# Cross attention's keys and the memory's norm made during setup, between the first modulation's quarters

## The chip, the cores and the metric

The kernel runs on one core of a Trainium2 chip. The metric is the device time of one launch in microseconds. The engines are TensorE (PE), VectorE (DVE), ScalarE (ACT), GpSimd (POOL) and SyncE (SP), which here only issues DMAs.

## The reference

A batch of one sequence with S = 512 tokens and D = 1024 channels goes through two transformer blocks and then a third one of another kind:

- Block 0: modulated RMS norm, a sparse attention mixer (NSA), a squared-ReLU MLP. Block 1: the same with a sliding-window attention. The modulation is `mod = silu(c) @ ada_w[i] + ada_b[i]`, cut into shift, scale and gate twice: `h = rms_norm(x) * (1 + scale) + shift`.
- Second part: `x += hybrid_mixer(rms_norm(x))`, `x += cross_attention(rms_norm(x), m)`, `x += conv_ffn(rms_norm(x))`, and a last norm.

What the change is about is the first modulation and this:

```
m = rms_norm_2(mem, norm_mem_w)            # mem: 256 rows of 1024, an input
q = h @ wq;  k, v = split(m @ wkv)         # 4 heads of 256
probs = softmax(q k^T * 256**-0.5);  x += (probs v) @ wo
```

`m`, `k` and `v` depend on inputs alone, not on x.

## The kernel before, in words

Activations lie transposed: channels on partitions in DC = 8 chunks of 128, tokens along the row. Every projection is made in float32 accuracy from two float32r parts. Weights come in units of 128 output channels x 1024 (512 KB). For each unit SP fetches `raw` (`units`, the transfer at L626), ACT makes the high part `wh` (L2634, `highs`), POOL the low part `wl` (L808), and PE makes three products a chunk: high x high, low x high, high x low (`products`, L915 to L917): 24 matmuls. `raw`, `wh` and `wl` are rings of RING = 4 slots. Results go to PSUM banks 0 to 3 in turn and are read out by DVE or ACT; the order of units is fixed by the list STAGES (L41). Every engine runs its own list in order, and semaphores (`wait_ge`, `then_inc`) tie them together. A wait on SP, ACT or POOL holds everything listed behind it.

**Setup.** SP loads positions, constants, x, and the 16 pieces of the first modulation's weights (each 128 input channels x 1024, for shift and for scale) before and around the first four units (L686 to L698). PE makes half of the scale with 128x128 weights and one moving column (`scale_part`, L1284); DVE accumulates the other half and the shift, 1024 columns an operation (L1879 to L1895); PE sums the partitions with a column of ones. ACT squares x, PE sums the squares (`square_sums`), and PE spreads the inverse root over the partitions (`root_spread`). DVE makes the rotary angles (`angle`), ACT their sines. Then the first norm: DVE scales a chunk (L1772), ACT adds the shift and rounds it to the high part `ah` (L2693), DVE makes the low part `al` (L1790). PE takes the chunks as they come, for three units at once (`gemm_first`, L969, which stores at L978, L979, L983); from the fourth unit on it goes unit by unit.

**Mixer's output and cross attention.** The memory (`me`, 1 MB) is fetched during the mixer's output projection (`gemm_squared` of mix_out, L1464). Its norm stands between that projection's units in four engines (`memory` in the PE, DVE and ACT lists): squares on ACT, sum on PE, root on ACT, scaling on DVE, high part `mh` on ACT, low part `ml` on DVE. Then PE makes the keys `xk`, one unit at a time with 256 columns: two around the residual's sum of squares, five after it, then three pairs of units with the memory as the weights (`gemm_pairs`: values `xv`), then the last key. Beside them DVE and ACT make the norm of x for the queries (`norm("xq", ...)`, L1772 and L1788). The query units follow; the last two value units are made inside the heads' loop.

Of the kernel before, what the change touches and what calls it, by code (L numbers as in the profile page):

```python
# [13 lines left out]
P = 128  # L14
# [21 lines left out]
UNITS_KV = 16  # L36
# [4 lines left out]
STAGES = (("nsa_in", UNITS_NSA_IN), ("phi", UNITS_PHI), ("nsa_out", UNITS_OUT), ("mlp0", UNITS_MLP),  # L41
          ("swa_in", UNITS_SWA_IN), ("swa_out", UNITS_OUT), ("mlp1", UNITS_MLP),
          ("mix_in", UNITS_MIX_IN), ("mix_out", UNITS_OUT), ("xq", UNITS_Q), ("kv", UNITS_KV),
          ("xo", UNITS_OUT), ("ffn", UNITS_FFN))
FIRST = {}
_n = 0
for _name, _count in STAGES:
# [5 lines left out]
SMALL = (("ones", P), ("ident", P), ("prev", P), ("diag", P), ("cmp_add", SC * P),  # L53
         ("inv", 1), ("cT", DC), ("ada_b", 96), ("norm_g", 64), ("pe", 32), ("b1", 4), ("b2k", 1), ("b2v", HD),
         ("w2", 4 * HD), ("sinks", HEADS), ("norm_mix", DC), ("norm_xattn", DC), ("norm_mem", DC),
         ("norm_ffn", DC), ("norm_final", DC), ("pool_scale", 4), ("gk_b", 2), ("gla_norm", 1),
         ("conv_w", 3 * 44), ("conv_b", 44), ("pool_w", 4 * P), ("gk_w2", 256), ("invcnt", 4 * 16),
         ("tri", HD), ("quarter", 4))
# [15 lines left out]
def place_of_units():  # L74

    n = {name: FIRST[name] for name, _ in STAGES}
    of = list(range(UNITS))

    def stage(name, runs):
        got = [n[name] + a + k for a, count in runs for k in range(count)]  # L80
        of[n[name]:n[name] + len(got)] = got
# [7 lines left out]
    xattn = n["xq"]  # L89
    kv = n["kv"]  # L90
    of[xattn:xattn + UNITS_KV + UNITS_Q] = [*range(kv, kv + 13), kv + 15, *range(n["xq"], n["xq"] + UNITS_Q), kv + 14, kv + 13]
# [5 lines left out]
KV0, XQ0 = FIRST["xq"], FIRST["xq"] + UNITS_KV - 2  # L97
# [155 lines left out]
def build(nc, src, out):  # L253
# [105 lines left out]
    trscr = scratch("trscr", [P, 2, S])  # L359

# [27 lines left out]
    me = at("me", 48, [P, DC, MEM])  # L388
    mh = at("mh", w0 + 16, [P, DC, MEM], F32R)
    ml = at("ml", w0 + 24, [P, DC, MEM], F32R)  # L390
    msq = at("msq", w0 + 54, [P, DC, MEM])
# [25 lines left out]
    ada_in = [sem(f"ada_in{i}") for i in range(16)]  # L417
    first_in = sem("first_in")
    scale_part_made = sem("scale_part_made")
    scale_sum = sem("scale_sum")  # L420
    shift_made = sem("shift_made")
    cond_done = sem("cond_done")
    ada_first = sem("ada_first")
# [99 lines left out]
    gla_std = sem("gla_std")  # L523
    mem_sq = sem("mem_sq")
# [25 lines left out]
    NORMS = ("nsa_in", "mlp0", "swa_in", "mlp1", "mix_in", "mem", "xq", "ffn_plain", "ffn")  # L550
# [13 lines left out]
    MEM_CHUNKS = {4: (0, 1, 2), 5: (3, 4, 5), 6: (6, 7)}  # L564
# [18 lines left out]
    def first_place(c):  # L583
        return ps[:, (7, 3, 4)[c % 3]]
# [31 lines left out]
    def _(sp):  # L616
        early = slice(COL["inv"][0], COL["cT"][1])
        sp.dma_start(sm[:, early], src["small"][:, early]).then_inc(first_in, 16)
        sp.dma_start(pos_i[:], src["pos"]).then_inc(first_in, 16)
# [66 lines left out]
        for n in (0, 8):  # L686
            sp.dma_start(ada0[:, n], src["ada"][n]).then_inc(ada_in[n], 16)
        for part in (slice(0, early.start), slice(early.stop, SMALL_COLS)):
            sp.dma_start(sm[:, part], src["small"][:, part]).then_inc(small_in, 16)
        for n in (1, 9):  # L690
            sp.dma_start(ada0[:, n], src["ada"][n]).then_inc(ada_in[n], 16)
        sp.dma_start(x[:], src["xT"]).then_inc(x_in, 16)
        for n in (10, 2, 11, 3, 12, 13, 14, 15):
            sp.dma_start(ada0[:, n], src["ada"][n]).then_inc(ada_in[n], 16)
        units(0, 1)
        for n in (4, 5, 6, 7):
            sp.dma_start(ada0[:, n], src["ada"][n]).then_inc(ada_in[n], 16)
        units(1, RING)  # L698
# [6 lines left out]
        units(RING, 10)  # L705
# [9 lines left out]
        units(10, 11)  # L715
        sp.wait_ge(kc_kept, 16 * GROUPS)
        load_tokens(0)
        for n in range(2):
            sp.wait_ge(evac, 2 + n + 1)
            for i in range(2):  # L720
                sp.dma_start(cscr[1, 2 * n + i], vtmp[64 * i:64 * i + 64, n]).then_inc(vc_kept, 16)
        units(11, 12)
        sp.wait_ge(vc_kept, 16 * GROUPS)
        load_tokens(1)
        units(12, 14)
        store_k(0, 0)
        units(14, 16)
        store_k(1, 1)
        units(16, 18)
        store_q(2, 0)  # L730
        units(18, 22)
        store_q(3, 1)
        units(22, 26)
        store_q(4, 2)
        units(26, 30)
# [6 lines left out]
        units(30, 32)  # L742
# [3 lines left out]
        units(32, FIRST["nsa_out"] + RING)  # L746
# [21 lines left out]
        sp.wait_ge(t_made, 3 * DC)  # L768
# [35 lines left out]
    def _(pool):  # L804
# [53 lines left out]
        def low_of_norm(name, shift, c, high=ah, to=al):  # L858

            if shift:  # L860
                pool.wait_ge(shifted, len(POOL_LOWS) * NORMS[1:].index(name) + c // 2 + 1)
            else:
                pool.wait_ge(high_made, DC * NORMS.index(name) + c + 1)
# [36 lines left out]
    def _(pe):  # L900
# [68 lines left out]
        def gemm_first(first, high, low, name, between=None):  # L969
# [3 lines left out]
            pe.wait_ge(lo_done, first + 3)  # L973
            for k in range(DC):
                pe.wait_ge(high_made, DC * NORMS.index(name) + k + 1)
                for j in range(3):
                    o, slot = ps[:, (n + j) % RING], (first + j) % RING
                    nc.tensor.matmul(o, wh[:, slot, k], high[:, k], start=k == 0, stop=False)  # L978
# [36 lines left out]

        def square_sum(c, tokens=S):

            q = squares[0]
# [2138 lines left out]
```

## Time and profile before

| | us |
|---|---|
| median of 3 runs | 2034.01 (2033.76 to 2034.55) |
| the profiled execution's own time | 2034.94 |
| its span | 2033.1 |
| PE busy | 1969.2 (97%) |
| DVE busy | 1133.1 (56%) |
| POOL busy | 942.7 (46%) |
| ACT busy | 702.1 (35%) |

The span is the time from the first to the last recorded instruction; the execution's own time is a little longer. PE's busy time counts pipelined matmuls whose ends are modelled, so a busy PE need not be at its peak: how far apart matmuls start tells more. Between stages the DMA engines move 124 GB/s on average.

### The profile page before, as it was taken

The page shows a single profiled execution, that of the slowest core. Times are in us where ns is not written, and L with a number is a line of the kernel's source. Part 1 is how long each engine was busy: PE and PEld are TensorE (multiplying, and loading weights), DVE is VectorE, ACT ScalarE, POOL GpSimd, SP SyncE. Part 2 cuts the span into 40 slices and gives each one's busy share as a digit, 9 for nine tenths or more (in the row PEclk, how much of TensorE's full clock was granted, in tenths as well). Part 3 has the DMA queues.
Part 4 walks back from the last instruction along what each step waited for, and adds up shares of the span by engine and source line. Part 5 has one row for each costly group of instructions (what it writes and reads, how often), then busy time and mean ns, then how long its engine had stood idle before and what let it go on. Part 6 is the DMA issues. An engine that isn't in the chain of part 4 may idle for free.

```text
span 2033.1 us, 27246 instructions
## 1 busy us (share of the span) xinstructions
PE 1969.2 (97%) x10389; PEld 1625.4 (80%) x10389; DVE 1133.1 (56%) x1763; ACT 702.1 (35%) x1230; POOL 942.7 (46%) x552
## 2 busy tenths in 40 slices
PE   6999999999999999999999999999999999999998
PEld 5888776878888887877888888788897788888887
DVE  7575785873645567766322313786463368345164
ACT  3343564432222233554322223342343342222122
POOL 1465554465444445564544444542363245444442
PEclk9998999999999999999999999999999999999999
DMA  7775340645555523722332332222343223332331
GB/s 291 233 218 169 98 121 26 224 145 190 201 179 196 176 73 114 208 93 63 110 98 93 100 98 93 73 73 73 100 137 95 63 73 114 94 103 93 94 103 63
DMA packets 81590, 252.24 MB, mean 124 GB/s; under 512 B 12224, under 2 KB 14784, under 8 KB 81216
## 3 DMA queue, kind: packets, MB, share of 16 engines
q1 hardware_dynamic: 81472, 250.61, 38.2%
q8 instruction: 80, 1.31, 0.3%
q14 instruction: 38, 0.31, 0.0%
HBM read 235.21 MB, written 15.37 MB: 123 GB/s over the span
## 4 chain that ended last, share of the span: by engine, by line
PE 73%; issue 12%; POOL 7%; DVE 5%; ACT 3%; POOLq 0%; DVEq 0%; ACTq 0%
PE ps L915 20%; PE ps L916 20%; PE ps L917 20%; POOL wl L808 5%; PE ps L1201 2%; PE ps L1141 2%; ACT pr L2781 2%; PE ps L1173 1%; DVE st L1996 1%; PE ps L1478 1%; PE ps L1503 1%; POOL al L864 1%; PE ps L983 1%; POOL x L856 1%; PE ps L963 0%
## 5 line engine op out<-in xcount | busy, mean ns | idle before, releaser
L808 POOL TENSOR_TENSOR wl<-raw,wh 128x1024 fp32r<-128x1024 f32 x309 | 768.8, 2493 | 943.1 <-ACT wh L2634 942.8
L2634 ACT CAST wh<-raw 128x1024 fp32r<-128x1024 f32 x309 | 322.4, 1050 | 899.3 <-PE ps L917 832.4
L915 PE MATMUL ps<-ah,wh 128*128 128x512 f32 x904 | 357.5, 395 | 1.3 <-DVE pair L1926 1.3
L916 PE MATMUL ps<-ah,wl 128*128 128x512 f32 x904 | 352.7, 390 | 0.0
L917 PE MATMUL ps<-al,wh 128*128 128x512 f32 x904 | 352.5, 390 | 0.0
L915 PE MATMUL ps<-hh,wh 128*128 128x512 f32 (+1 forms) x712 | 273.2, 384 | 2.0 <-DVE hl L2537 2.0
L916 PE MATMUL ps<-hh,wl 128*128 128x512 f32 (+1 forms) x712 | 272.1, 382 | 0.0
L917 PE MATMUL ps<-hl,wh 128*128 128x512 f32 (+1 forms) x712 | 272.0, 382 | 0.0
L915 PEld LDWEIGHTS ps<-ah,wh 128*128 128x128 f32 x904 | 170.3, 188 | 40.0 <-issue 2.6
L916 PEld LDWEIGHTS ps<-ah,wl 128*128 128x128 f32 x904 | 170.2, 188 | 35.9 <-issue 1.5
L917 PEld LDWEIGHTS ps<-al,wh 128*128 128x128 f32 x904 | 170.1, 188 | 35.8
L915 PEld LDWEIGHTS ps<-hh,wh 128*128 128x128 f32 x712 | 133.8, 188 | 29.8 <-DVE hl L2537 3.3
L917 PEld LDWEIGHTS ps<-hl,wh 128*128 128x128 f32 x712 | 133.9, 188 | 26.1
L916 PEld LDWEIGHTS ps<-hh,wl 128*128 128x128 f32 x712 | 133.9, 188 | 25.5
L915 PE MATMUL ps<-fh,wh 128*128 128x512 f32 x328 | 127.6, 389 | 0.0
L916 PE MATMUL ps<-fh,wl 128*128 128x512 f32 x328 | 127.6, 389 | 0.0
L917 PE MATMUL ps<-fl,wh 128*128 128x512 f32 x328 | 127.6, 389 | 0.0
L2781 ACT ACTIVATE pr<-ps,st 128x512 f32<-128x512 f32 (+1 forms) x192 | 94.0, 503 | 55.7 <-DVE st L1996 45.8
L2158 DVE TENSOR_SCALAR rs<-ps 128x512 f32<-128x512 f32 x64 | 44.1, 690 | 114.7 <-PE ps L917 109.7
L827 POOL TENSOR_SCALAR pr<-pr,st,gates 128x512 f32<-128x512 f32 (+3 forms) x128 | 81.0, 647 | 56.3 <-DVE st L2024 56.2
L1141 PE MATMUL ps<-ks,qs 128*128 128x256 f32 (+3 forms) x384 | 89.3, 340 | 5.6 <-ACT pr L2781 3.6
L2171 DVE TENSOR_TENSOR y<-ps,y 128x512 f32<-128x512 f32 x32 | 22.1, 691 | 125.7 <-PE ps L917 125.7
(419 smaller groups left out, 3270.2 us busy)
## 6 DMA issues: line engine op xcount, KB each, us to landing
raw<-in_units SPq DMA_DIRECT2D x309, 512.0 KB, 3.6
ada_mlp<-in_ada SPq DMA_DIRECT2D x64, 512.0 KB, 3.3
ada<-in_ada SPq DMA_DIRECT2D x16, 512.0 KB, 15.8
qs<-qscr SPq DMA_DIRECT2D x32, 256.0 KB, 3.3
ada_in<-in_ada SPq DMA_DIRECT2D x16, 512.0 KB, 3.7
ks<-kscr SPq DMA_DIRECT2D x24, 256.0 KB, 4.6
x<-in_xT SPq DMA_DIRECT2D x1, 2048.0 KB, 13.8
qscr<-rot_h SPq DMA_DIRECT2D x16, 128.0 KB, 2.3
```

The source lines that it names most:

```text
L808: nc.gpsimd.tensor_tensor(wl[:, slot], raw[:, slot], wh[:, slot].bitcast(F32), ALU.subtract).then_inc(lo_done, 1)
L827: op = nc.gpsimd.tensor_scalar(o, o, st[:, 2, n % 4, i:i + 1], gates[:, i, c:c + 1], ALU.mult, ALU.mult)
L856: nc.gpsimd.tensor_tensor(x[:, c], y[:, c], x[:, c], ALU.add).then_inc(x_new_pool, 1)
L915: nc.tensor.matmul(out_ap, wh[:, slot, k], high[:, k0 + k], start=first and k == 0, stop=False)
L916: nc.tensor.matmul(out_ap, wl[:, slot, k], high[:, k0 + k], start=False, stop=False)
L917: mm = nc.tensor.matmul(out_ap, wh[:, slot, k], low[:, k0 + k], start=False, stop=last and k == ks - 1)
L1141: nc.tensor.matmul(o, qs[:, Q_SLOT[j], i * P:(i + 1) * P], ks[:, slot, part, k0 * P:k1 * P], start=part == 0, stop=False)
L1201: mm = nc.tensor.matmul(ps[HD * h:HD * h + HD, bank, q[0] * P:(q[-1] + 1) * P], vv[:, kind, kb, col_v:col_v + HD], pt[:, n[h] % 4, place[k ...
L2158: link(v.tensor_scalar(rs[:, k % 2], b, 0.0, None, ALU.max))
L2171: v.tensor_tensor(y[:, c], bank(), y[:, c], ALU.add).then_inc(evac, 1)
L2634: a.copy(wh[:, slot], raw[:, slot]).then_inc(hi_done, 1)
L2781: a.activation(pr[:, n % 3, b * S + col:b * S + col + width], ps[:, plan.s_bank(w, b), col:col + width], ACT.Exp, bias=shift[:, i:i + 1], ...
```

## The change

- Units are reordered: stage `xk` (8 key units) comes first of all, ahead of `nsa_in`; only the 8 value units stay in cross attention.
- The table of constants is reordered, so that the first piece holds all that setup needs, and the memory is the second transfer.
- The memory's norm and the keys are made in setup, with the same operations as before, half of the squares now on DVE. Highs and lows of the memory (`mh0`, `ml0`) and the keys (`xk0`) are stored to DRAM (`mscr`, `xkscr`), and fetched back during mix_out.
- The first modulation is made otherwise: by quarters of 256 output channels, wholly on PE (`condition`): four input chunks side by side on column groups of 32, twice accumulated. ACT copies the bank (`rows`), PE transposes it (`turn_rows`), DVE adds the four parts (`first_coefs`). Quarters 0 and 1 stand between keys 4 and 7, quarters 2 and 3 inside the first group of the NSA gemm. The quarter's weights are fetched as runs of 256 floats.
- x's squares are summed by DVE (`first_square`) and once on PE, instead of chunk by chunk on PE.
- `gemm_first` of the first stage waits for its three units one by one.
- In cross attention `values` makes a pair of value units in two halves of 128 memory rows; the first pair stands around the residual's sum of squares.

```diff
@@ STAGES
+STAGES = (("xk", UNITS_K), *LAID[:10], ("xv", UNITS_V), *LAID[11:])
@@ SP, setup (the old order of loads is gone)
+        def ada_load_first(q):
+
+            if q == 3:
+                sp.wait_ge(rows_made, 1)
+            for w in (1, 0):
+                sp.dma_start(ada0[:, q % 3, w], src["ada"][DC * w:DC * w + DC, :, 256 * q:256 * q + 256].rearrange("k p m -> p k m")
+                             ).then_inc(ada_in[2 * q + w], 16)
+        units(0, 3)
+        sp.dma_start(pos_i[:], src["pos"]).then_inc(pos_in, 16)
+        sp.dma_start(x[:, 0:4], src["xT"][:, 0:4]).then_inc(x_half, 16)
+        sp.dma_start(x[:, 4:8], src["xT"][:, 4:8]).then_inc(x_in, 16)
+        units(3, 6)
+        ada_load_first(0)
+        units(6, 7)
+        ada_load_first(1)
+        units(7, NSA0 + 1)
+        ada_load_first(2)
+        nsa_units(1, 3)
+        ada_load_first(3)
+        nsa_units(3, 4)
+        for part, tile in enumerate((mh0, ml0)):
+            sp.dma_start(mscr[part], tile[:].bitcast(F32)).then_inc(mem_kept, 16)
+        sp.dma_start(sm[:, early.stop:], src["small"][:, early.stop:]).then_inc(small_in, 16)
+        nsa_units(4, 5)
         sp.wait_ge(trig_made, 2)
         sp.dma_start(trscr, ang[:, 4:6]).then_inc(trig_kept, 16)
+        sp.wait_ge(evac, UNITS_K)
+        sp.dma_start(xkscr, xk0[:]).then_inc(mem_kept, 16)
+        nsa_units(5, 6)
 
         sp.wait_ge(trig_kept, 16)
-        sp.wait_ge(t_made, DC)
+        sp.wait_ge(t_made, 2 * DC)
...
@@ SP, mix_out
-        units(FIRST["swa_out"] + RING, FIRST["mix_out"] + 6)
-        sp.wait_ge(pooled, 4)
-        sp.dma_start(me[:], src["memT"]).then_inc(x_in, 16)
-        units(FIRST["mix_out"] + 6, UNITS)
+        units(FIRST["swa_out"] + RING, FIRST["mix_out"] + 8)
+        sp.wait_ge(head_made, 4)
+        for part, tile in enumerate((mh, ml)):
+            sp.dma_start(tile[:].bitcast(F32), mscr[part]).then_inc(mem_back, 16)
+        units(FIRST["mix_out"] + 8, FIRST["mix_out"] + 12)
+        sp.wait_ge(unit_used, FIRST["mix_out"] + UNITS_OUT)
+        sp.dma_start(xk[:], xkscr).then_inc(keys_back, 16)
+        units(FIRST["mix_out"] + 12, UNITS)
@@ PE, setup
+        def condition(q):
+
+            for w in (1, 0):
+                pe.wait_ge(ada_in[2 * q + w], 16)
+                if q and w:
+                    pe.wait_ge(rows_read, q)
+                for r in range(2):
+                    for j in range(4):
+                        k = 4 * r + j
+                        mm = nc.tensor.matmul(ps[32 * j:32 * j + 32, 6, 256 * w:256 * w + 256],
+                                              cond[:, k:k + 1].to_broadcast([P, 32]), ada0[:, q % 3, w, k],
+                                              start=r == 0, stop=r == 1)
+            mm.then_inc(rows_made, 1)
+        def next_rows(k):
+
+            q = k // 2 + 2
+            if q < 4 and k % 2:
+                turn_rows(q)
+            elif q < 4:
+                condition(q)
...
+        for j in range(4):
+            keys(j)
+        sums_squared(spread_too=False)
+        keys(4)
+        root_spread(1)
         pe.wait_ge(cond_done, 1)
-        for k in range(2):
-            scale_part(k)
-        pe.wait_ge(setup_done, 1)
-        square_sums()
...
+        condition(0)
+        keys(5)
+        turn_rows(0)
+        keys(6)
+        condition(1)
+        keys(7)
+        turn_rows(1)
         u = FIRST["nsa_in"]
-        gemm_first(u, ah, al, "nsa_in")
+        gemm_first(u, ah, al, "nsa_in", between=next_rows, one_by_one=True)
@@ PE, cross attention
-        gemm_squared(FIRST["mix_out"], oh, ol, ready=(evac, done[0] - 8), between=memory)
-
-        gemm(KV0 + 2, 5, mh, ml, tokens=MEM)
-        gemm_pairs(KV0 + 7, 3, mh, ml, tokens=MEM)
-        gemm(KV0 + 13, 1, mh, ml, tokens=MEM)
+        def first_values(c):
+
+            if c == DC - 1:
+                pe.wait_ge(mem_back, 32)
+                values(V0, 0)
+            if c == DC:
+                values(V0, 1)
+        gemm_squared(FIRST["mix_out"], oh, ol, ready=(evac, done[0] - 8), between=first_values)
+
+        for pair in (1, 2):
+            for i in range(MC):
+                values(V0 + 2 * pair, i)
@@ DVE, setup
+        key_out(0)
         for step in range(4):
-            angle(0, step)
-        angle(1, 0)
...
+            angle(step // 4, step % 4)
+        key_out(1)
+        first_square(2)
+        first_square(3)
+        key_out(2)
+        for c in range(4, DC):
+            first_square(c)
+        sets[0] += 1
+        summed[0] += 1
+        key_out(3)
+        rms(1)
+        for step in range(4, 8):
+            angle(step // 4, step % 4)
+        key_out(4)
+        key_out(5)
@@ ACT, setup
+        highs(0, 1)
+        act.wait_ge(mem_sum, 1)
+        a.activation(rs[0:64, 0, 0:P], ps[0:64, 6, 0:P], ACT.Sqrt, bias=eps[0:64], scale=1.0 / D).then_inc(std_made, 1)
+        highs(1, 2)
+        for k in range(DC):
+            act.wait_ge(t_made, k + 1)
+            a.copy(mh0[:, k], me[:, k]).then_inc(high_made, 1)
+        normed[0] += 1
+        highs(2, 3)
+        for c in range(4):
+            first_square(c)
+        highs(3, 4)
+        for c in range(4, DC):
+            first_square(c)
+        summed[0] += 1
+        highs(4, 5)
+        act.wait_ge(sq_used, squared[0])
+        a.copy(sxx[:], ps[:, 4, 0:P])
+        root(1)
+        act.wait_ge(first_in, 16)
+        a.activation(cond[:], small("cT"), ACT.Silu).then_inc(cond_done, 1)
+        highs(5, 6)
         act.wait_ge(ang_done, 2)
         for h in range(2):
             a.activation(ang[:, 4 + h], ang[:, 4 + h], ACT.Sin).then_inc(trig_made, 1)
+        highs(6, 7)
+        keep_rows(0)
+        highs(7, 8)
+        for q in range(4):
+            act.wait_ge(shift_made, q + 1)
+            for c in (2 * q, 2 * q + 1):
+                act.wait_ge(t_made, DC + c + 1)
+                a.activation(ah[:, c], first_place(c), ACT.Identity, bias=mod[:, c:c + 1]).then_inc(high_made, 1)
+            if q == 0:
+                highs(8, 9)
+            if q < 3:
+                keep_rows(q + 1)
+            if q == 0:
+                highs(9, 11)
+        normed[0] += 1
+        highs(11, 12)
```

## Rows read from the trace of the kernel before

**Rows 1.** The page's busy times: share of the span and instructions.

```profile
PE 1969.2 (97%) x10389; PEld 1625.4 (80%) x10389; DVE 1133.1 (56%) x1763; ACT 702.1 (35%) x1230; POOL 942.7 (46%) x552
```

**Rows 2.** Busy time by stretch of setup: engine busy (instructions), granted clock, DMA share, GB/s.

```profile
30.00:44.00 14.00, 10.76 (x49) 10.50 (x49) 11.58 (x14) 4.97 (x6) 7.86 (x4) 1.00 0.67 267
44.00:63.00 19.00, 18.96 (x72) 15.47 (x73) 9.04 (x13) 4.49 (x7) 1.47 (x1) 1.00 0.36 139
```

**Rows 3.** Timeline of PE in setup: start, duration, line, operation, tiles, idle before.

```profile
37.58 3.57 PE L1094 MATMUL ps<-sm,acc 128*128 128x1 f32 x16 [0.21 <-DVE acc L1881]
...
44.60 0.63 PE L979 MATMUL ps<-ah,wl 128*128 128x512 f32 x1
45.03 0.63 PE L978 MATMUL ps<-ah,wh 128*128 128x512 f32 x1
...
61.62 0.39 PE L978 MATMUL ps<-ah,wh 128*128 128x512 f32 x1
61.84 0.39 PE L979 MATMUL ps<-ah,wl 128*128 128x512 f32 x1
...
63.20 0.39 PE L915 MATMUL ps<-ah,wh 128*128 128x512 f32 x1
```

**Rows 4.** x's load in the timeline, and the memory's load with its time to landing.

```profile
4.74 0.59 SPq L692 DMA_DIRECT2D x<-in_xT  x1
...
18.65 1.15 ACT L2644 ACTIVATE sq<-x 128x512 f32<-128x512 f32 x2 [14.41 <-DMA x<-in_xT]
...
me<-in_memT SPq DMA_DIRECT2D x1, 1024.0 KB, 5.6
```

**Rows 5.** Timeline of the memory's norm in the output projection (PE, ACT, DVE).

```profile
1445.70 1.32 ACT L2938 ACTIVATE msq<-me 128x256 f32<-128x256 f32 x4
1454.94 1.94 PE L998 MATMUL ps<-msq,sm 128*32 128x128 f32 x32
1456.69 1.28 ACT L2941 ACT_TABLE_LOAD   x1
1468.66 1.27 DVE L2436 SCALAR_TENSOR_TENSOR me<-me,sm,ps 128x256 f32<-128x256 f32 x3
```

**Rows 6.** Timeline of PE from the first key to the first query matmul.

```profile
1485.00 0.28 PE L915 MATMUL ps<-mh,wh 128*128 128x256 f32 x1
1485.11 0.28 PE L916 MATMUL ps<-mh,wl 128*128 128x256 f32 x1
...
1491.50 1.05 PE L1006 MATMUL ps<-rs,sm 128*128 128x128 f32 x8
1492.31 0.36 PE L915 MATMUL ps<-mh,wh 128*128 128x256 f32 x1
...
1527.48 0.40 PE L915 MATMUL ps<-ah,wh 128*128 128x512 f32 x1
```

**Rows 7.** Timeline of POOL and DVE in the query norm: POOL busy, then idle.

```profile
1490.05 21.21 POOL L808 TENSOR_TENSOR wl<-raw,wh 128x1024 fp32r<-128x1024 f32 x8 [6.70 <-ACT wh L2634]
...
1495.81 1.93 DVE L1788 TENSOR_TENSOR al<-tt,ah 128x512 fp32r<-128x512 f32 x1
...
1513.36 0.68 DVE L1788 TENSOR_TENSOR al<-tt,ah 128x512 fp32r<-128x512 f32 x1
```

**Rows 8.** The page's costliest groups: a unit's low and high.

```profile
L808 POOL TENSOR_TENSOR wl<-raw,wh 128x1024 fp32r<-128x1024 f32 x309 | 768.8, 2493 | 943.1 <-ACT wh L2634 942.8
L2634 ACT CAST wh<-raw 128x1024 fp32r<-128x1024 f32 x309 | 322.4, 1050 | 899.3 <-PE ps L917 832.4
```

**Rows 9.** Timeline of DVE in setup: first and last of eight angle operations.

```profile
5.02 0.43 DVE L1827 TENSOR_SCALAR ang<-ang 128x512 f32<-128x512 f32 x1
...
9.05 0.43 DVE L1840 TENSOR_SCALAR ang<-ang 128x512 f32<-128x512 f32 x1
```

**Rows 10.** Timeline of PE in the heads: four score matmuls, four transposes.

```profile
1539.33 1.99 PE L1478 MATMUL ps<-xk,xq 128*128 128x256 f32 x8 [0.78 <-DVE xq L2277]
1546.66 0.60 PE L1491 MATMUL ps<-sm,xp 128*128 128x128 f32 x4
```

More of the change, by code:

```diff
@@ L967, in gemm_pairs, with gemm_first @@
                 done[0] += tokens // P // 2
-        def gemm_first(first, high, low, name, between=None):
+        def gemm_first(first, high, low, name, between=None, one_by_one=False):
             n = done[0]
             bank_free(n + 2)
-            pe.wait_ge(lo_done, first + 3)
+            if not one_by_one:
+                pe.wait_ge(lo_done, first + 3)
             for k in range(DC):
@@ L977, in gemm_first @@
                     o, slot = ps[:, (n + j) % RING], (first + j) % RING
+                    if one_by_one and k == 0:
+                        pe.wait_ge(lo_done, first + j + 1)
                     nc.tensor.matmul(o, wh[:, slot, k], high[:, k], start=k == 0, stop=False)
@@ L1297, in _ @@
-        root_spread(1)
-        pe.wait_ge(scale_part_made, 4)
-        for m in range(8):
-            mm = nc.tensor.matmul(ps[:, 7, m:m + 1], acc1[:, m * P:(m + 1) * P], small("ones")[:, 0:1],
-                                  start=False, stop=m == 7)
-        mm.then_inc(scale_sum, 1)
-        pe.wait_ge(ada_first, 8)
-        ada(ps[:, 6, 0:8], acc0)
+        def condition(q):
[10 more added lines that the diff above has]
+            mm.then_inc(rows_made, 1)
@@ new lines, in turn_rows, with keys @@
+        def turn_rows(q):
+            pe.wait_ge(rows_kept, q + 1)
+            for i in range(4):
+                mm = nc.tensor.transpose(ps[:, 6, i * P:(i + 1) * P], rows[:, q % 2, i * P:(i + 1) * P], small("ident"))
+            mm.then_inc(rows_turned, 1)
+        def next_rows(k):
[4 more added lines that the diff above has]
+                condition(q)
+        def keys(j):
+            gemm(j, 1, mh0, ml0, tokens=MEM, ready=None if j else A_READY["mem"])
@@ L1527, in _ @@
             else:
-                last_values(0)
+                values(LAST_VALUES, 0)
             xturn(h, 0)
@@ L1909, in _, with first_coefs, part @@
-        norm("nsa_in", x, coef_at(0, 0), coef_at(0, 1), ah, al, root=False, after=first_shift, place=first_place)
+        def first_coefs(q):
+            def part(t):
+                return t.rearrange("p (w c) -> p w c", w=2)[:, :, 2 * q:2 * q + 2]
+            dve.wait_ge(rows_turned, q + 1)
+            turned = ps[:, 6].rearrange("p (w c f) -> p w c f", w=2, c=2)[:, :, :, 0:P:32]
+            v.tensor_reduce(part(mod[:, 0:16]), turned, X, ALU.add).then_inc(rows_read, 1)
+            dve.wait_ge(rows_read, q + 1)
+            v.tensor_tensor(part(mod[:, 0:16]), part(mod[:, 0:16]), part(small("ada_b")[:, 0:16]), ALU.add).then_inc(shift_made, 1)
+            dve.wait_ge(shift_made, q + 1)
+            link(v.scalar_tensor_tensor(out=coef[:, 0, 0, 2 * q:2 * q + 2], in0=mod[:, 8 + 2 * q:10 + 2 * q], scalar=1.0,
+                                        in1=small("norm_g")[:, 2 * q:2 * q + 2], op0=ALU.add, op1=ALU.mult))
@@ L2635, in highs, with first_square @@
             over_units(act, first, min(last, UNITS), high)
-        def squares(chunk, wait):
-            for c in range(DC):
-                act.wait_ge(*wait)
-                if c >= 2:
-                    act.wait_ge(sq_used, squared[0] - 1)
-                a.activation(sq[:, c % 2], chunk[:, c], ACT.Square).then_inc(sq_made, 1)
-                squared[0] += 1
+        def first_square(c):
+            act.wait_ge(x_half if c < 4 else x_in, 16)
+            if c >= 3:
+                act.wait_ge(sq_added, c - 2)
+            a.activation(sq[:, c % 2] if c else ps[:, 4], x[:, c], ACT.Square).then_inc(sq_made, 1)
+            squared[0] += 1
         def root(slot, tokens=S):
```

384 lines of the change are left out of this document (176 added, 208 removed).

## The prediction

> **What bounds the kernel now.** I read the busy shares first: PE is busy 97% of the span [rows 1], so an edit gains only where it takes PE work off or fills one of PE's few holes. The table of stretches shows where the holes are: the setup. From 30 to 44 us PE counts as busy, but on 49 small instructions, and DVE is busy 11.58 of the 14 us; between 44.0 and 63.2 us stands the first real matmul group, 72 matmuls on the first three units [rows 2, 3]. Second, the timeline of PE there: the first matmuls of 512 columns start 0.43 us apart, later ones 0.22 [rows 3]. 512 columns in 0.43 us is the 1.2 GHz level, in 0.22 the 2.4 GHz level, although the granted clock of that stretch reads 1.00 [rows 2]; before it stood 14 us of PE work with one moving column each. The unit after the group starts at 63.20 [rows 3]. That is my reference point at the front. At the back, the timeline of PE in cross attention: keys and values run without a hole from 1485.00 to the first query matmul at 1527.48 [rows 6].
>
> **Removed at the back.** A key unit is 24 matmuls of 256 columns, 0.12 us apart [rows 6]: 2.87 us, eight of them 23.0. They filled the time of the residual's sum and root; now the first value pair does that, 48 matmuls of the same size, one half ahead of the sum and one behind it. After 1485.00: values 2.9, sum 0.8, values 2.9, spread 0.8 (1491.50 to 1492.31 [rows 6]), two more pairs 11.7. The query gemm can start at 1504.1 instead of 1527.48: 23.4 us. The memory's sum of squares goes too (1454.94 to 1456.81, 1.9 us with the change of kind [rows 5]) and its spread, half as many instructions as the full one: 0.5. Together 25.8.
>
> Is something else late at 1504? The cross norm needs 8 x 2 DVE operations of some 0.7 us and one value eviction, from 1492.6: 1504.5 if undisturbed. But the lows of that norm read two SBUF tiles, and while POOL makes a unit's low they take 1.93 us, against 0.68 when it is idle [rows 7]. The Trainium skill ("SBUF — State Buffer", on the engine side of the ports) gives this as a lock: a VectorE instruction with two SBUF inputs waits for a GpSimd instruction that reads SBUF. The trace agrees, with 1.93 against 0.68. Four POOL lows remain in that stretch (units 5, 6 of the values, two of the queries; 2.4 us each); I put three or four DVE lows behind one each, so the last is done at about 1509. PE consumes one chunk in 0.68 us, so it wants the last at 1508.9: no more than 0.5 lost. The transfers: SP now waits until the whole output projection is used (1485.0) and fetches the keys (1 MB, 5.6 us for the memory's load of that size [rows 4]) ahead of the fifth value unit. That lands at about 1492; its slot is free at 1491.6 anyway. Low of the sixth at 1498.3, where PE wants it at 1498.2. Cost 0 to 1.5. I take 25.5 for the back; bounds 26, and 22 if each of the eight lows meets a POOL instruction (2.5 more) and the transfer costs its 1.5.
>
> **Added in front, and its chain.** The setup's transfers are read at 0.41 MB/us: x is behind 3.7 MB (four modulation pieces 2.1, tables 1.4, positions 0.3), itself 2.1 MB, and is there at 18.65 [rows 4]: 5.8 MB in 14.1 us, with 3 us of start and 1.5 of completion. Small table and memory (1.4 MB) are there at about 8.0, units 0 to 2 at 9 to 12, x at 17.5, first modulation quarter 26, second 33. Step by step, each at the price of before's rows:
> - Squares 1.3 (four on ACT, four on DVE) [rows 5]: 9.4. Sum on PE 1.94 [rows 5], twice that at the low level: 13.1. Root 0.4, reciprocal 1, spread 0.6, semaphores: 16.
> - Eight scalings and eight lows of 256 columns at 0.42 [rows 5]: 22.5; key 0 follows chunk by chunk and ends then.
> - ACT: the high of unit 2 stands behind the memory's eight highs: 22.7, its low (2.49 [rows 8]) 25.2. Key 2 ends 28.3.
> - DVE: two operations on the positions, one key eviction and eight angle operations from 22.4, the eight of the first half 4.5 us, from 5.02 to the end of the last at 9.48 [rows 9]: 28.3. x's square 3 waits for DVE's first addition (29.4), unit 3's high comes behind that square: 31.0, low 33.4. PE sits idle 28.3 to 33.5.
> - Key 3, again partly at the low level: 38.0. Sum, root 39.5, table load 1.28 [rows 5] and Silu: 41.0. Key 4 41.5, spread 42.5.
> - A condition: 4 rounds of four column-tiled float32 matmuls with 256 columns. The memory's sum has eight rounds of 128 columns in 1.94 [rows 5], so 0.24 and for 256 columns 0.48: 1.9 a condition. If the tiles don't overlap it is 16 x 0.50, by the scores of 256 columns (4 in 1.99 [rows 10]): 8.0. I take 1.9: it is the row with the same tiling. It ends 44.4.
> - Unit 5's high comes behind Silu (42), its low 44.1 to 46.5, held by DVE's three angle operations that read two SBUF tiles (the lock again; without it key 5 is 2 us earlier, which the sines' wait mostly takes back); key 5 49.5; ACT's sines wait for the second angles (45.0), then unit 6's high and the first rows' copy (48); turn 0 (four transposes 0.60 [rows 10]) 50.1; key 6 52.9; condition 1 54.8; key 7 57.7; turn 1 58.3.
> - First group: unit 10's high stands behind the copy of rows 1, its low ends 61.7. Then one chunk at 2.04 (9 x 0.227), seven more 14.3, two conditions 3.8, two turns 1.2, handovers: 82.2. A quarter's coefficients, scaling and high (2.4 us after its turn) lie beside the chunk between.
>
> Against 63.2 that is 19.0 us later. In numbers of PE work: 23.0 of keys, 7.6 conditions, 2.4 turns come in; 14 us of one-column work and DVE's 1.29 us accumulations go out; and the first group no longer starts at the low level.
>
> What the rest of the edit costs: stores (memory 2 MB, keys 1 MB) and the late small table lie on SP behind unit 11, at 55 to 60, and nothing on the chain waits; unit 12 is wanted at 87. The rotary table's fetch waits for x's eighth scaled chunk (76) and lands before the first rotary at 82. The fetches in the projection have 40 us. Zero for all, up to 1 if unit 12 or 13 queues behind them.
>
> **Sum.** 19.0 - 25.5 = -6.5. Profiled execution: span 2033.1, its time 2034.9; it would be 2028.4. The median of the runs shown is 0.9 lower than that execution: 2034.0 - 6.5 = 2027.5.
>
> Bounds of the front: from key 0's end at 22.5 the pure PE work is 20.1 + 1.7 + 7.6 + 2.4 + 16.3 = 48.1, so not before 70.6 (+7.4); with all steps at the high level the chain gives 78.5 (+15.3); with the low level again after each hole of 1 us or more, 86 (+23); conditions without overlap would add 24.
>
> **Rivals.**
> A, the setup packs well: the high level from key 1, POOL never waited for. Front +10 to +15, back 25.5: -10 to -15, 2021. For it: key 1 and 2 are dense. Against it: five ACT-POOL handovers of 3.5 us (1.04 + 2.49 [rows 8]) stand on the chain.
> B, nothing in sum: front +22 to +25: 2032 to 2034. For it: every link of the chain above is a handover between four engines, and one more wait in each of three engines makes 4 us.
> C, slower: PE stays at the 1.2 GHz level until the first group begins, as it did before 44 us and for some 5.7 us into the group [rows 3]. Keys 1 to 7 then cost 5.1 each instead of 2.87, conditions 3.8. Carried through the same chain the group ends at 91 to 93: +28 to +30 against 25.5, so +3 to +4, 2038; through the group as well it would be 100 and +11. It decides from 88.7 on. For it: the hole 28 to 33. Against it: from 33.5 on no hole in my chain is longer than 2.1 us, and in cross attention the same matmuls run at the high level [rows 6]. The Trainium skill ("TensorE: Matmul & The Clock Gate", on the HAM clock gate) says that the low level is the default and that sustained activity releases it; so it too would have the keys pay at their start and after the hole.
> D, the modulation's transfers: runs of 1 KB where they were 4 KB. No transfer of before has such runs. At 0.41 MB/us they are 8 us ahead of need; at half that the chain ends 4 us later, at a third it is the bound and the change is slower by 8. The Trainium skill ("DMA: Bandwidth & Descriptors", specifications) asks for 512 B a descriptor for full rate, so by it nothing is lost.
>
> **Chances.** The forecast (front +16.5 to +22, so -9 to -3.5) 0.5; A 0.2; B 0.17; C 0.08; D or something else that makes it slower 0.05. From the measurement 0.2%, 4 us, can be told from nothing. Faster by more: A and about four fifths of the forecast, and a bit of B: 0.64; within 0.23; slower 0.13. Range: 2019.5 (between A's end and the floor) to 2036 (C's beginning); the forecast's own is 2025 to 2030.5.
>
> **What would show it.** In the changed kernel: memory keys' matmuls between 16 and 58 us with one hole of about 5 us before key 3, released by POOL's low; condition groups of 1.9 us, four; the unit after the first group near 82 (before 63.20). In cross attention the first query matmul 19.1 us behind the first value matmul, where keys to queries took 42.5; the values' matmuls without a wait on DMA. Query matmuls that wait for DVE lows by over 2 us, keys 0.21 us apart from 34 us on, or conditions of 8 us would make it wrong.

## The result, and the profile after

| | before | after |
|---|---|---|
| median, same chip (lowest to highest of 18 runs each) | 2034.51 (2032.80 to 2038.43) | 2038.66 (2036.65 to 2042.27) |
| the profiled execution's own time | 2034.94 | 2042.27 |
| its span | 2033.1 | 2040.5 |
| PE busy | 1969.2 | 1967.3 |

The changed kernel is slower: ratio 1.0017, 95% interval 1.0010 to 1.0024, about 3.5 us. Forecast were 6.5 us less. The profiled execution of after is the slowest of its 18 runs: the two traces lie 7.3 us apart, twice the 3.5 us of the ratio. Where the surplus lies is seen below by comparing stretches over all traces.

| milestone on PE | before | after | forecast |
|---|---|---|---|
| unit after the first group | 63.20 | 86.48 (+23.3) | +19.0 |
| from there to the first key (before) or first value (after) | 1421.80 | 1422.39 | 1419.4 (memory's sum and spread gone) |
| from there to the first query matmul | 42.48 | 19.40 | 19.1 |
| first query matmul to first scores | 11.85 | 18.80 | 12.4 |
| first scores to the end of the span | 493.8 | 493.4 | same |

Three rows miss: the front by 4.3 us, the middle by 3.0, and the query units by 6.4.

The middle holds two things. The output projection, in which the memory's norm stood, took 47.59 us before (1437.41 to 1485.00) and 44.65 after (1464.22 to 1508.87):

```profile
1437.41 0.39 PE L915 MATMUL ps<-oh,wh 128*128 128x512 f32 x1
```

```profile
1464.22 0.39 PE L957 MATMUL ps<-oh,wh 128*128 128x512 f32 x1
```

That is 2.9 us less, where 2.4 was forecast, and it is within 0.05 us of that in every trace of this document. What lies ahead of the projection took 1374.2 us before and 1377.7 after. Over all traces it takes 1373.6 to 1377.9 us with the new order and 1374.2 to 1376.9 with the old one, so these 3.5 us are no shown effect of the change.

The timeline of PE in cross attention, after (start, duration, line, operation, tiles, number, and in brackets the idle time before and what ended it), answers to [rows 6, 10]:

```profile
1508.87 0.28 PE L1525 MATMUL ps<-wh,mh 128*128 128x256 f32 x1
...
1528.27 0.40 PE L957 MATMUL ps<-ah,wh 128*128 128x512 f32 x1
...
1534.17 0.50 PE L957 MATMUL ps<-ah,wh 128*128 128x512 f32 x1 [1.62 <-DVE al L1850]
...
1536.93 0.79 PE L957 MATMUL ps<-ah,wh 128*128 128x512 f32 x1 [1.78 <-DVE al L1850]
1537.52 0.63 PE L958 MATMUL ps<-ah,wl 128*128 128x512 f32 x1
...
1547.07 1.97 PE L1553 MATMUL ps<-xk,xq 128*128 128x256 f32 x8 [0.88 <-DVE xq L2372]
```

The query gemm starts where it should. Its seventh and eighth chunks wait 1.62 and 1.78 us for DVE's low parts, and from 1536.93 on the matmuls start 0.43 us apart instead of 0.23 until 1542.6. The next table (stretch, its length, busy time and instructions of PE, weight load, DVE, ACT, POOL, then granted clock, DMA share, GB/s) shows the level: 0.50, which is 1.2 GHz.

```profile
1537.00:1541.00 4.00, 4.00 (x10) 3.13 (x11) 1.16 (x2) 1.04 (x1) 1.21 (x1) 0.50 0.43 131
```

That makes 3.4 us of waits and 2.8 us of matmuls at half rate (14 x 0.2). What DVE and POOL did there, to be read against [rows 7]:

```profile
1518.88 1.22 DVE L1850 TENSOR_TENSOR al<-tt,ah 128x512 fp32r<-128x512 f32 x1 [0.35 <-ACT ah L3051]
...
1520.79 2.12 DVE L1850 TENSOR_TENSOR al<-tt,ah 128x512 fp32r<-128x512 f32 x1
...
1523.61 0.69 DVE L1850 TENSOR_TENSOR al<-tt,ah 128x512 fp32r<-128x512 f32 x1
...
1529.20 7.67 DVE L1850 TENSOR_TENSOR al<-tt,ah 128x512 fp32r<-128x512 f32 x3
```

```profile
1525.38 5.40 POOL L850 TENSOR_TENSOR wl<-raw,wh 128x1024 fp32r<-128x1024 f32 x2 [3.02 <-ACT wh L2710]
1530.97 5.36 POOL L850 TENSOR_TENSOR wl<-raw,wh 128x1024 fp32r<-128x1024 f32 x2 [0.18 <-ACT wh L2710]
```

The last three lows take 2.56 us each in the mean. PE's chunks start at 1534.17 and 1536.93, each 0.5 to 0.6 behind the end of a POOL low (1533.65, which is 1530.97 plus half of 5.36, and 1536.33). POOL pays too: 2.70 a low, where [rows 8] have 2.49 in the mean.

The front, timeline of PE after, answers to [rows 3]:

```profile
32.73 0.58 PE L957 MATMUL ps<-mh,wh 128*128 128x256 f32 x1 [5.57 <-POOL wl L850]
...
33.33 0.41 PE L959 MATMUL ps<-ml,wh 128*128 128x256 f32 x1
33.54 0.41 PE L957 MATMUL ps<-mh,wh 128*128 128x256 f32 x1
...
42.53 1.93 PE L1326 MATMUL ps<-ada,cond 128*32 128x256 f32 x32
...
49.25 0.66 PE L1335 MATMUL ps<-sm,rows 128*128 128x128 f32 x4 [1.60 <-ACT rows L2810]
...
51.28 0.43 PE L957 MATMUL ps<-mh,wh 128*128 128x256 f32 x1 [1.38 <-POOL wl L850]
...
55.81 1.93 PE L1326 MATMUL ps<-ada,cond 128*32 128x256 f32 x32
...
64.19 0.50 PE L1023 MATMUL ps<-ah,wh 128*128 128x512 f32 x1 [1.57 <-POOL wl L850]
...
65.90 3.18 PE L1326 MATMUL ps<-ada,cond 128*32 128x256 f32 x32
...
86.48 0.39 PE L957 MATMUL ps<-ah,wh 128*128 128x512 f32 x1
```

Key 3 comes after a hole of 5.6 us at 0.21 us apart. A condition is 1.93 us, the third 3.18. Key 6 waits for POOL's low and takes 4.5 us (51.28 to 55.81). DVE and POOL near there:

```profile
42.20 2.74 DVE L1896 SCALAR_TENSOR_TENSOR ang<-ang 128x512 f32<-128x512 f32 x1
44.98 0.69 DVE L1898 SCALAR_TENSOR_TENSOR ang<-ang 128x512 f32<-128x512 f32 x1
...
51.19 2.28 DVE L1977 SCALAR_TENSOR_TENSOR coef<-mod,sm 128x2 f32<-128x2 f32 x1
```

```profile
41.79 2.60 POOL L850 TENSOR_TENSOR wl<-raw,wh 128x1024 fp32r<-128x1024 f32 x1 [5.37 <-ACT wh L2710]
```

The same operation on the same tile takes 2.74 us beside POOL's low and 0.69 after it. The coefficients, two values a partition, take 2.28.

### The profile page after: what moved, and what is told of

Read it like the earlier page. It is cut to its first block, busy times and chain, and to the rows that moved or that the text cites. A ratio compares the mean times of both kernels' runs of the same rounds, so it can differ in the third digit from the quotient of the medians.

```text
span 2040.5 us, 27258 instructions
## 1 busy us (share of the span) xinstructions
PE 1967.3 (96%) x10389; PEld 1616.4 (79%) x10389; DVE 1129.9 (55%) x1769; ACT 703.6 (34%) x1231; POOL 943.9 (46%) x552
## 4 chain that ended last, share of the span: by engine, by line
PE 78%; DVE 8%; issue 6%; POOL 4%; ACT 3%; DMA 0%; POOLq 0%; DVEq 0%; SPq 0%; ACTq 0%
PE ps L957 21%; PE ps L958 21%; PE ps L959 21%; POOL wl L850 3%; PE ps L1234 2%; PE ps L1174 2%; ACT pr L2894 1%; PE ps L1206 1%; PE ps L1553 1%; DVE st L2092 1%; PE ps L1028 1%; PE ps L1578 1%; DVE al L1850 1%; PE ps L1023 1%; PE ps L1024 1%
```

## The experiments

Theory: the back lost 6.4 us because DVE's lows of the query norm, which read two SBUF tiles, stand behind POOL's lows; the front is a chain of handovers in which the same lock, and PE's 1.2 GHz level after each hole, cost 4 us more than forecast. Lock means here that a DVE operation with two SBUF inputs waits while POOL works. Rivals: DVE or ACT simply have more to do; PE's own work sets the setup's length; the costs belong to one execution.

Times are compared by the ratio to the kernel before on the same chip; the changed kernel has 1.0017. "Group's end" is the start of the unit after the first group (after: 86.48). The group is three weight units; PE starts them one by one, in the changed kernel at 61.00, 61.88 and 64.19, and the third condition follows the third.

**e1, the query norm's scaled chunks in PSUM.** Only where a chunk lies changes, so DVE's low reads one SBUF tile and one PSUM bank.

```diff
+    def query_place(c):
+        return ps[:, (6, 7, 4)[c % 3]]
-        norm("xq", x, small_at("norm_xattn"), None, ah, al, beside=...)
+        norm("xq", x, small_at("norm_xattn"), None, ah, al, beside=..., place=query_place)
-            a.copy(ah[:, c], tt[:, c % 3]).then_inc(high_made, 1)
+            a.copy(ah[:, c], query_place(c)).then_inc(high_made, 1)
```

> The changed kernel, but the query norm's scaled chunks lie in PSUM banks 6, 7 and 4 instead of SBUF, so that its lows read one SBUF tile. Lock theory (DVE's low waits for POOL's unit low because both read SBUF): the lows take 0.7 us each, the last is done before 1509 + shift, the two waits of the first query unit (1.6 and 1.8 us) and the spell at the 1.2 GHz level behind them (2.8 us) go; about 6.5 us faster than the changed kernel, so near 2032. Rival (the DVE list of the norm is simply too long for two value pairs as cover, or the weights come late): the waits stay within 1 us of what they were and the time stays at 2038 to 2039.

Measured: 2032.62 us, ratio 0.9980 (0.9971 to 0.9989): 7.5 us below the changed kernel. DVE's lows and a pair of POOL's in its trace, and PE's start of the values and of the scores:

```profile
1515.92 0.69 DVE L1853 TENSOR_TENSOR al<-ps,ah 128x512 fp32r<-128x512 f32 x1 [0.23 <-ACT ah L3055]
...
1523.45 1.88 DVE L1853 TENSOR_TENSOR al<-ps,ah 128x512 fp32r<-128x512 f32 x3
```

```profile
1520.74 4.78 POOL L853 TENSOR_TENSOR wl<-raw,wh 128x1024 fp32r<-128x1024 f32 x2 [1.76 <-ACT wh L2714]
```

```profile
1506.02 0.28 PE L1528 MATMUL ps<-wh,mh 128*128 128x256 f32 x1
...
1537.07 1.97 PE L1556 MATMUL ps<-xk,xq 128*128 128x256 f32 x8 [0.88 <-DVE xq L2375]
```

The lows take 0.63 to 0.69 us while POOL is at work, POOL's own 2.39, and values to scores take 31.05 us instead of 38.20 (36.69 in e9's trace): 5.6 to 7.2 us, within the noise of the 7.5 of the ratios. The lock theory holds, and this one term turns the change from slower to faster than before.

**e6, the same edit in the kernel before.** The control: is it the change that uncovered the lock?

> The kernel before, with only e1's edit: the query norm's scaled chunks in PSUM. Theory (the lock cost before nothing, because PE was in the keys and values until 1527.48 while the norm's last low was done at 1514; the change uncovered it): DVE's lows fall from 1.93 to about 0.7 us there too, the norm ends about 8 us earlier, and the time doesn't move: ratio 0.9995 to 1.0005. Rival (the copy from PSUM is worth something by itself, wherever it stands): ratio 0.998 or less, as in e1, 0.9980.

Measured: 2036.67 us beside 2037.32, ratio 0.9995 (0.9986 to 1.0004). The lows fall to 0.68 us, and keys to queries take 42.49 us (1487.08 to 1529.57), as before (42.48). One part of the expectation was wrong: the norm doesn't end earlier, since in the kernel before its lows alternate with the evictions of the keys, and the last is not at 1514 but at 1525.4, still 6 us ahead of its chunk. The first and last low of this run:

```profile
1497.89 0.68 DVE L1791 TENSOR_TENSOR al<-ps,ah 128x512 fp32r<-128x512 f32 x1
...
1527.49 0.68 DVE L1791 TENSOR_TENSOR al<-ps,ah 128x512 fp32r<-128x512 f32 x1
```

The edit is worth nothing that can be told under cover, and 5.6 to 7.2 us of PE's time without it.

**e2, unit 3's high ahead of x's square 3** (on ACT in setup).

```diff
-        for c in range(4):
+        for c in range(3):
             first_square(c)
         highs(3, 4)
+        first_square(3)
```

> The changed kernel, but ACT makes the high of unit 3 ahead of x's square 3, which waits for DVE's first addition behind the angles. Chain theory (setup is a chain of handovers, and key 3 waits for that high): PE's hole of 5.8 us before key 3 shrinks to under 1, the spell at the 1.2 GHz level in key 3 goes too, but root and Silu depend on the squares as before, so of it 2 to 4 us reach the end: 2035 to 2037. Rival (the setup is bound by PE's own work): the hole moves to the next wait, and the time stays at 2038 to 2039.

Measured: 2036.72 us, ratio 1.0002 (0.9993 to 1.0011); group's end 83.91. The hole before key 3 goes, and two new ones come, first for the squares' sum, then for unit 4's low:

```profile
34.57 0.42 PE L1043 MATMUL ps<-tt,sm 128*32 128x128 f32 x8 [4.29 <-DVE tt L1911]
...
37.95 0.55 PE L957 MATMUL ps<-mh,wh 128*128 128x256 f32 x1 [2.74 <-POOL wl L850]
```

**e3, the sines behind unit 7's high** (ACT no longer waits for the angles ahead of unit 6's high).

```diff
-        act.wait_ge(ang_done, 2)
-        for h in range(2):
-            a.activation(ang[:, 4 + h], ang[:, 4 + h], ACT.Sin).then_inc(trig_made, 1)
         highs(6, 7)
         keep_rows(0)
         highs(7, 8)
+        act.wait_ge(ang_done, 2)
+        for h in range(2):
+            a.activation(ang[:, 4 + h], ang[:, 4 + h], ACT.Sin).then_inc(trig_made, 1)
```

> The changed kernel, but ACT's two sines come behind the highs of units 6 and 7 and the first copy of rows. Chain theory: unit 6's high no longer waits for the second half of the angles (46.6 us), key 6 starts some 3 us earlier, and the clock spell in it goes: 2 to 4 us faster than the changed kernel, 2035 to 2037. Rival (something behind it, the fourth quarter or POOL's lows of units 9 and 10, is the bound of the first group): under 1 us.

Measured: 2036.69 us, ratio 1.0008 (0.9999 to 1.0017); group's end 84.94. The group's first matmul comes 3.9 us earlier (57.10 instead of 61.00, line L1023), but its lows are not there: the third unit's comes 2.5 earlier (61.64 instead of 64.19). There PE falls to the low level, and stays at it in the third condition:

```profile
59.32 0.50 PE L1023 MATMUL ps<-ah,wh 128*128 128x512 f32 x1 [1.51 <-POOL wl L850]
61.64 0.80 PE L1023 MATMUL ps<-ah,wh 128*128 128x512 f32 x1 [1.59 <-POOL wl L850]
64.08 3.46 PE L1326 MATMUL ps<-ada,cond 128*32 128x256 f32 x32
```

Group's end alone is inconclusive: e1, whose setup is the changed kernel's, also has 84.94 in its trace. The move gained 2.5 us at the third unit, and the low level took 1.0 us of it back (23.3 us from there to group's end, 22.3 in the changed kernel).

**e4, the rounded turns of the angles in PSUM** (`ang[:, 2]` becomes `ps[:, 7]` in `angle`).

> The changed kernel, but the rounded turns of the angles lie in PSUM bank 7 instead of SBUF, so that the three angle operations with two inputs read one SBUF tile. Lock theory: no angle operation is longer than 0.9 us (in the changed kernel the first was 1.77 and one of the second half 2.74), the angles end 1 and 2 us earlier, and since both stand on the chain, 2 to 3 us come off: 2036. Rival (the long ones are waits for something else): they stay long, and the time is 2038 to 2039.

Measured: 2036.25 us, ratio 1.0003 (0.9994 to 1.0012); group's end 82.50, 4.0 us earlier: 2.4 at the second unit's first matmul (59.51 instead of 61.88), 1.2 in the third condition, which stays at the high level. Only the 2.4 can be put down to the edit, since e1, with the changed kernel's setup, has the third condition at the high level too. The angle operation that had 2.74 us, beside a POOL low again (40.62 to 42.99), and the coefficients, which were left as they were:

```profile
41.89 0.69 DVE L1896 SCALAR_TENSOR_TENSOR ang<-ps,ang 128x512 f32<-128x512 f32 x1
...
48.83 2.29 DVE L1977 SCALAR_TENSOR_TENSOR coef<-mod,sm 128x2 f32<-128x2 f32 x1
```

**e8, the hole filled.** 40 matmuls behind key 2, result unused.

```diff
+            if j == 2:
+                for k in range(40):
+                    nc.tensor.matmul(ps[:, 7, 0:MEM], mh0[:, k % 8, 0:P], mh0[:, k % 8], start=k == 0, stop=k == 39)
```

> 40 more matmuls of 256 columns, whose result nobody uses, on the memory's high part behind key 2: they fill the hole of 5.7 us (27.0 to 32.7) in which PE waits for unit 3's low. Theory (key 3 runs 0.21 us apart because PE stood idle before it): key 3's matmuls are 0.12 apart and it ends 2 to 2.4 us earlier (35.6 to 36); what follows (sum, root, Silu, condition) moves by as much only where DVE and ACT are done, so the unit after the first group moves by 0 to 2.4. Rival (the rate of key 3 has another cause, such as waiting chunk by chunk or the other engines' traffic): 0.21 apart as before.

Measured: 2036.33 us, ratio 1.0002 (0.9992 to 1.0012). Key 3 starts at the same time, now 0.12 us apart:

```profile
26.59 4.96 PE L1358 MATMUL ps<-mh 128*128 128x256 f32 x40
32.82 0.39 PE L957 MATMUL ps<-mh,wh 128*128 128x256 f32 x1 [1.27 <-POOL wl L850]
33.04 0.28 PE L958 MATMUL ps<-mh,wl 128*128 128x256 f32 x1
33.16 0.28 PE L959 MATMUL ps<-ml,wh 128*128 128x256 f32 x1
```

It is done at 35.8 instead of 38.0, and group's end is 82.75, 3.7 us earlier, more than the expected 2.4 at most: 2.1 us reach the second unit's first matmul (59.75 instead of 61.88), and the third condition then takes 1.93 us instead of 3.18. The 2.1 are within what was expected; the rest, as in e4, isn't shown to come from the edit. Five microseconds more of PE work made the kernel no slower (the ratio is 3 us lower, with intervals that overlap). Behind the hole the clock's level costs PE 2.2 us in key 3, which the edit takes away.

**e7, one chunk of eight in the keys.** Leaves out seven eighths of the keys' products, 20 us of PE work at the high level.

```diff
-            gemm(j, 1, mh0, ml0, tokens=MEM, ready=None if j else A_READY["mem"])
+            gemm(j, 1, mh0, ml0, tokens=MEM, ks=1, ready=None if j else A_READY["mem"])
```

> Leaves out seven of the eight input chunks of each key's product: 3 matmuls a key instead of 24, so PE has 8 x 21 x 0.12 = 20.2 us less work in setup (4.8 more at the low level by the same count); everything else stands. Theory (the setup is a chain of handovers: the high and low of each unit, the sum's and the roots' way, the turns): most of that work stood beside a wait for ACT, POOL or DVE; the unit after the first group comes 5 to 10 us earlier, at 77 to 82. Rival (PE's own work sets the setup's length, so that my sum failed by its matmuls' rate): 18 us or more earlier, at 66 to 68.

Measured: 2036.54 us, ratio 0.9998 (0.9989 to 1.0007), 3.9 us below the changed kernel; group's end 82.10, 4.4 earlier, even less than the theory's 5 to 10:

```profile
32.52 0.58 PE L957 MATMUL ps<-mh,wh 128*128 128x256 f32 x1 [8.33 <-POOL wl L850]
...
45.18 0.66 PE L1335 MATMUL ps<-sm,rows 128*128 128x128 f32 x4 [3.43 <-ACT rows L2810]
...
55.09 0.47 PE L1023 MATMUL ps<-ah,wh 128*128 128x512 f32 x1 [1.29 <-POOL wl L850]
57.31 0.80 PE L1023 MATMUL ps<-ah,wh 128*128 128x512 f32 x1 [1.51 <-POOL wl L850]
```

The work became waits for the same lows and rows. The setup is a chain of ACT, POOL and DVE in which the keys fill holes.

**e5, the four edits together** (e1, e2, e3, e4).

> The edits of e1 to e4 together: the query norm's scaled chunks in PSUM, unit 3's high ahead of x's square 3, the sines behind unit 7's high, the rounded turns of the angles in PSUM. Alone they put the unit after the first group 1.6 (sines), 2.6 (unit 3) and 4.0 us (angles) earlier than the 86.6 of the changed kernel, and e1 gave 7 us at the back. Theory (the front is a chain of handovers, each edit takes a different link): the three add up in good part, the unit after the first group at 79 to 81, first value matmul to first scores 31.1 as in e1, the time 12 to 14 us below the changed kernel, ratio to the kernel before 0.995 to 0.996. Rival (one next link, POOL's low or PE's own work, binds behind each of them): the unit after the first group at 82 to 83, no better than the angles alone, ratio 0.9965 or more.

Measured: 2024.62 us beside 2037.32, ratio 0.9936 (0.9922 to 0.9949), that is 13 us below the kernel before and 16.5 below the changed one; the best of all. Group's end 78.48, values to scores 31.05:

```profile
57.81 0.50 PE L1026 MATMUL ps<-ah,wh 128*128 128x512 f32 x1 [1.57 <-POOL wl L853]
...
78.48 0.39 PE L960 MATMUL ps<-ah,wh 128*128 128x512 f32 x1
```

At group's end the front edits come to 8.0 us against 2.6, 1.5 and 4.0 singly, but the level in the third condition is part of each of these. At the third unit's first matmul, ahead of that condition, they give 6.4 us together (57.81 instead of 64.19) and 2.6, 2.5 and 2.4 singly: they add up in good part, as the theory had it.

**e9, the changed kernel again.**

> The changed kernel itself once more, with a second trace: how much of its +23.3 in front and of the +3.5 in the middle (between the first group's end and the mixer's output) belongs to one execution. Theory (they vary with PE's clock after short waits): the unit after the first group between 84.9 (as in e1 and e3) and 86.5, the stretch from there to the first value matmul 1418 to 1422 against 1422.4; first value matmul to first scores again 38.2, since the locked lows stand there every time; ratio 1.001 to 1.0025. Rival (they are fixed costs of the change): 86.5 and 1422.4 again.

Measured: 2039.94 us beside 2035.20, ratio 1.0018 (1.0009 to 1.0027). Group's end 86.21 (its third condition 3.00 us), from there to the values 1422.0, values to scores 36.7: the locked lows stand as before (again 7.66 us for the last three), but the spell at the low level behind them cost 1.5 us less. The expectation's 38.2 missed by that. With e1's setup at 84.94, the change's cost in front is 21.7 to 23.3 us by execution. The middle stretch lay between 1418.2 (e3) and 1422.5 (e2) in the traces that keep the new order, with no edit in it.

All traces of the new order side by side, in us. "Between" is the difference of the two columns before it; it separates what an edit moved from what PE's level in the group gave or took.

| trace | third unit's first matmul | group's end | between | values to scores |
|---|---|---|---|---|
| changed kernel | 64.19 | 86.48 | 22.3 | 38.20 |
| e9, the same again | 63.93 | 86.21 | 22.3 | 36.69 |
| e1, query norm in PSUM | 64.26 | 84.94 | 20.7 | 31.05 |
| e2, unit 3 first | 61.61 | 83.91 | 22.3 | 38.13 |
| e3, sines later | 61.64 | 84.94 | 23.3 | 36.89 |
| e4, angles in PSUM | 61.82 | 82.50 | 20.7 | 36.89 |
| e8, hole filled | 62.06 | 82.75 | 20.7 | 36.89 |
| e7, one chunk of eight | 59.63 | 82.10 | 22.5 | 37.89 |
| e5, all four | 57.81 | 78.48 | 20.7 | 31.05 |

Two things can be read from it. With the group's PE work all at the high level "between" is 20.7; a low spell adds 1.6 to 2.6. And in the seven traces that keep the scaled chunks in SBUF, values to scores take 36.7 to 38.2, in the two with them in PSUM 31.05.

## Why the prediction was wrong

**The mechanism of the gain was right.** Values to the first query matmul 19.4 us, forecast 19.1; no value matmul of PE waited for a transfer; conditions 1.93, forecast 1.9, so their four tiles overlap; keys 0 to 2 dense, the hole before key 3 5.6 us long (forecast 5.2) and released by POOL's low, key 3's end 38.0 and the spread 42.5 as forecast to the tenth. The tenth is luck: key 3 began 0.8 us earlier than forecast (32.7 for 33.5) and ran longer. The memory's norm gave 2.9 us, forecast 2.4.

**The step that failed: "no more than 0.5 lost"** to the query norm's lows. It cost 6.4 more than the 0.5 in the changed trace, 4.9 in the second one. Three things in it were off. The count: I put three or four of the eight lows behind a POOL instruction, six were. I counted four POOL lows in that stretch, with two query units; but the ring of four slots had room for four query units, and from 1525.38 to 1536.33 POOL had only 0.2 us of rest. The price: I took 1.93 against 0.68 from [rows 7] as the cost of a lock, but POOL worked back to back there too (eight lows in 21.21 us, 2.65 each). Before, a DVE low also got through about once a POOL instruction: they started 2.8 to 3.0 us apart. Only a part of that shows in their durations, 1.68 to 1.93, because between two of them DVE had a scaling and a key's eviction to do, 0.75 and 0.42 us, which didn't wait:

```profile
1497.77 0.75 DVE L1772 SCALAR_TENSOR_TENSOR tt<-x,sm,ps 128x512 f32<-128x512 f32 x1
1498.44 0.41 DVE L2277 COPY xk<-ps 128x256 f32<-128x256 f32 x1
1498.77 1.78 DVE L1788 TENSOR_TENSOR al<-tt,ah 128x512 fp32r<-128x512 f32 x1
```

In the changed kernel the last three lows stand one behind the other, with nothing between them, and each takes 2.56. The eight lows cost 13.9 us together, where my count makes 9 to 10. And what follows a wait: 3.4 us of waiting were followed by another 2.8 lost at 1.2 GHz (1.3 in e9), a term that my sum for the back didn't have. My outer bound for the back, 22, had all eight lows locked, but at 1.93 and without the clock; measured were 19.1 in the changed trace (54.33 less 38.20, and 2.9 of the memory's norm) and 20.6 in e9's.

The Trainium skill ("SBUF — State Buffer", section "SBUF: two separate sides") gives the lock between VectorE with two SBUF inputs and GpSimd reading SBUF. e1 and e6 agree: 2.56 us with two SBUF inputs, 0.63 with one in PSUM, beside the same POOL work. The rule was cited in the prediction; the error was to price it by a duration from a stretch where DVE had other work between its lows.

**The second term, the front: 19.0 forecast, 21.7 to 23.3 measured.** The chain's times hold until turn 0 (forecast end 50.1, measured 49.9), but at turn 0 by luck. I had the lock slow POOL's low of unit 5 and end key 5 at 49.5; POOL's low took 2.60 us, DVE's angle operation paid, key 5 ended at 47.7, and turn 0 then waited 1.6 us for ACT's rows behind the sines. The step "key 6 52.9" failed: key 6 had to wait for POOL's low, which stood behind the angles, the sines and unit 6's high, and PE at the low level took 4.5 us for it: 55.8. The angles before it ended at 46.6, forecast 45.0. From there everything is 2.9 later. Another 1.2 is the third condition at the low level. The lock on the angles (2.74 against 0.69) stood in the forecast; I gave it 2 us "which the sines' wait mostly takes back", e4 measured 2.4 at the third unit. One reading of before was loose as well: of the 14 us that I called one-column work [rows 2], that work filled 9, spreading the root 2, and PE had nothing for 2.9 just before the group.

**The rivals.** A (packs well): not as the change stands, but e5 reaches +15.3 in front, A's edge. B (nothing) came closest in front, +22 to +25, while it kept the back at 25.5. C has the right number, 2038, by another way, so that is luck: it said that PE would stay at 1.2 GHz, front +28 to +30; PE fell to it only in spells, behind waits, and e8 shows it for one: fill the hole of 5.6 us and key 3 runs at 0.12. The clock's price stands on both sides: key 3 2.4 us (1.6 of them in the forecast), key 6 1.7 and the third condition 1.2 (not in it), 1.3 to 2.8 at the back (not in it). The Trainium skill ("TensorE: Matmul & The Clock Gate", section "Part 1: The HAM clock gate") lets sustained activity release the clock, and the traces agree, with key 3 at 0.21 and 0.12 us. D fell: with the runs of 1 KB of the first two quarters on their way, from 20 to 30 us, the DMA engines moved 351 GB/s, and PE waited for none of them.

**The sum.** Forecast 19.0 - 25.5 = -6.5. By the traces, front 21.7 to 23.3; back 19.1 to 20.6 (54.33 less 38.20 or 36.69, and 2.9 for the memory's norm): +1.1 to +4.2, and the measured ratios, 1.0017 and 1.0018, are +3.5 us. The range ended at 2036, and even the back's bound of 22 with a front of 23.3 would have stayed below it (+1.3, so 2035.8): what went past it is the 1.4 to 2.9 us by which the back fell short of its own bound.

## What to carry to other kernels

When a cover is moved away, price what it had covered by the stretch to come: how many instructions of the other engine will stand there back to back, and how much other work the waiting engine has between its own. The duration of one instruction, read in a stretch with such other work, is too small. An intermediate of a DVE operation that runs beside POOL belongs in PSUM where a bank is free; here two such edits and two moves on ACT turned +3.5 us into -13. In this chain of handovers PE's holes cost twice, as a wait and as the clock behind it, so that work which fills them is nearly free and work taken out of them brings little.

## What the runs showed of the hardware

- The lock meets small and simple operations too. Coefficients of two values a partition took 2.28 us beside POOL and 0.16 in e5 where POOL was idle (its lows end at 47.2 and run again from 50.6). In e5 also an operation with a single SBUF input and SBUF output took 2.28 against 0.43:

```profile
38.91 2.28 DVE L1904 TENSOR_SCALAR ang<-ang 128x512 f32<-128x512 f32 x1
...
47.27 0.16 DVE L1980 SCALAR_TENSOR_TENSOR coef<-mod,sm 128x2 f32<-128x2 f32 x1
...
55.51 2.27 DVE L1980 SCALAR_TENSOR_TENSOR coef<-mod,sm 128x2 f32<-128x2 f32 x1
```

- The price of PSUM for that is small: the turns' roundings took 0.70 instead of 0.43 us there, the low 0.63 to 0.69 as in SBUF.
- Behind two waits of 1.6 and 1.8 us with three matmuls between them PE fell to 1.2 GHz in the query units, in all seven traces that have these waits; what the spell cost differed by 1.5 us between executions. In front one execution had its third condition at 1.93 us (e1), two at 3.0 and 3.2, with the same instructions.
